# A decoder trunk with expert retrieval: dot products against a PSUM copy of the tokens, and expert values scaled by ScalarE and summed by accumulating transposes

## The reference

```python
q = (xt @ w_q).reshape(t, 8, 2, 128)
s = einsum("thpd,hpnd->thpn", q, sub_keys)          # 128 keys on each of two sides
s1, i1 = top_k(s[:, :, 0], 16); s2, i2 = top_k(s[:, :, 1], 16)
top_s, pos = top_k(all 256 sums s1 + s2, 16)        # idx: 16 of 16384 experts per head
g = softmax(top_s)
a = einsum("cd,chkd->chk", xc, u_tab[idx])          # one dot product per token and expert
out = einsum("chk,chkd->cd", g * gelu(a), v_tab[idx])
```

## Time and profile before

| | |
|---|---|
| median of 3 runs | 1714.5 us (1711.46 to 1718.54) |
| the profiled execution: span from the first to the last instruction | 1705.4 us |
| of the span: TensorE busy | 1427.1 us (84%) |
| GpSimd busy | 1179.6 us (69%) |
| VectorE busy | 1003.6 us (59%) |
| ScalarE busy | 474.8 us (28%) |
| DMA | 619.30 MB, mean 363 GB/s |

### The profile page before, as it was taken

How to read it: one execution, slowest core, us unless ns; L and a number is a source line. 1 busy time by engine, 2 the same in 40 slices (tenths; PEclk the granted TensorE clock), 3 DMA queues, 4 the chain that set the end, 5 groups by cost and what they waited for, 6 DMA issues and landing times.

```text
span 1705.4 us, 18671 instructions
## 1 busy us (share of the span) xinstructions
PE 1427.1 (84%) x5274; PEld 813.2 (48%) x5274; DVE 1003.6 (59%) x2462; ACT 474.8 (28%) x1459; POOL 1179.6 (69%) x1099
## 2 busy tenths in 40 slices
PE   8999887888777899988787799989878877787775
PEld 7887544455442565454344466545444432233332
DVE  3257777767765534537777824654667864444444
ACT  0213233333232222432333321441333231111112
POOL 0027688777777756776777766786777787777774
PEclk9999999999999999999999999989999998999998
DMA  9629999999999999999999999999999999999997
GB/s 336 195 76 355 367 331 334 378 373 354 350 399 403 392 390 393 371 369 390 400 397 384 391 374 389 388 335 370 391 403 333 362 345 370 397 410 410 409 410 301
DMA packets 224237, 619.30 MB, mean 363 GB/s; under 512 B 18913, under 2 KB 90651, under 8 KB 224155
## 3 DMA queue, kind: packets, MB, share of 16 engines
q0 software_dynamic: 147456, 536.94, 82.1%
q1 hardware_dynamic: 76699, 81.36, 14.3%
HBM read 617.17 MB, written 1.05 MB: 363 GB/s over the span
## 4 chain that ended last, share of the span: by engine, by line
PE 35%; POOL 20%; issue 14%; DVE 13%; DMA 11%; ACT 6%; POOLq 1%; SPq 0%; DVEq 0%; ACTq 0%
PE acc L743 17%; PE tile L704 14%; POOL v_ring L483 10%; POOL u_ring L483 10%; DMA u_ring<-in_peer_u_dram,idx_now 9%; DVE u_ring L939 5%; ACT diag L564 3%; DMA v_ring<-in_peer_v_dram,idx_now 2%; ACT gelus L558 2%; PE tile L840 1%; PE tile L726 1%; PE tile L867 1%; DVE cand L1200 0%; DVE cand L1205 0%; DVE picked L1207 0%
## 5 line engine op out<-in xcount | busy, mean ns | idle before, releaser
L743 PE MATMUL acc<-v_ring,diag 128*128 128x512 f32 x2032 | 962.2, 625 | 147.5 <-DMA v_ring<-in_peer_v_dram,idx_now 101.3
L939 DVE CUSTOM_DVE_ANT_0 u_ring<-u_ring,xffn 128x1024 f32<-128x1024 f32 x512 | 605.6, 1222 | 273.1 <-DMA u_ring<-in_peer_u_dram,idx_now 272.3
L483 POOL DMA_INDIRECT v_ring<-in_peer_v_dram,idx_now x512 | 579.8, 1132 | 206.1 <-issue 127.1
L743 PEld LDWEIGHTS acc<-v_ring,diag 128*128 128x128 f32 x2032 | 392.2, 200 | 688.1 <-issue 670.6
L483 POOL DMA_INDIRECT u_ring<-in_peer_u_dram,idx_now x512 | 574.9, 1123 | 192.4 <-issue 131.7
L550 ACT ACTIVATE gelus<-dots 128x8 f32<-128x8 f32 x64 | 13.4, 209 | 783.3 <-DVE dots L939 783.3
L564 ACT ACTIVATE diag<-ident,gelus 128x128 f32<-128x128 f32 x512 | 156.5, 388 | 2.1
L704 PEld LDWEIGHTS tile<-fT,w_ring 128*128 128x128 f32 x960 | 113.8, 195 | 19.8 <-issue 11.0
L704 PE MATMUL tile<-fT,w_ring 128*128 128x128 f32 x960 | 114.7, 279 | 7.9 <-DVE fT L1065 7.9
L1171 DVE MAX8 topv<-tile 128x8 f32<-128x128 f32 x64 | 15.9, 290 | 165.3 <-PE tile L840 165.3
L558 ACT ACTIVATE gelus<-gelus,gates 128x1 f32<-128x1 f32 x512 | 102.0, 281 | 4.8 <-ACT gelus L550 3.1
(11 more groups left out here) (145 smaller groups left out, 953.4 us busy)
## 6 DMA issues: line engine op xcount, KB each, us to landing
w_ring<-in_peer_wq_dram SPq DMA_DIRECT2D x23, 1024.0 KB, 16.6
w_ring<-in_w_out_dram SPq DMA_DIRECT2D x12, 1024.0 KB, 19.3
w_ring<-in_w_kv_dram SPq DMA_DIRECT2D x12, 1024.0 KB, 16.6
u_ring<-in_peer_u_dram,idx_now POOLq DMA_INDIRECT x512, 7.2
v_ring<-in_peer_v_dram,idx_now POOLq DMA_INDIRECT x512, 7.1
w_ring<-in_w_in_b_dram SPq DMA_DIRECT2D x8, 1024.0 KB, 23.5
u_ring<-in_w_in_a_dram SPq DMA_DIRECT2D x4, 1024.0 KB, 12.6
w_ring<-in_w_mem_kv_dram SPq DMA_DIRECT2D x4, 1024.0 KB, 14.3
```

Of the source, the lines that this page charges most:

```text
L483: pool.indirect_dma_start(ring[:, s, :], None, rows_[:, :], bass.IndirectOffsetOnAxis(idx_now[:, column + s:column + s + 1], 0), element_o ...
L743: ins = pe.matmul(acc[:, 512 * n:512 * n + 512], diag[:, par * G + s, :], v_ring[:, s, 512 * n:512 * n + 512], start=False, stop=False, sk ...
L939: dve.tensor_tensor_reduce(u_ring[:, s, :], u_ring[:, s, :], xffn[:, ph % 2, :], 1.0, 0.0, ALU.mult, ALU.add, dots[:, par * G + s:par * G ...
```

## The change

Three things are changed together.

1. **Dot products.** At the start of a phase VectorE copies `xffn` into a PSUM tensor `xf` of two banks (`place_row`), and the 8 x 16 dots of the phase read `xf` instead of `xffn`. To make room, there are 4 `tile` banks instead of 6 from the first `ffn` step on; before that step `xf` serves as banks 4 and 5.
2. **Values.** ScalarE no longer writes `diag`. It waits for `v_landed[s]`, scales the whole v slot in place (128x1024), and TensorE adds it by 8 transposes of 128x128 which accumulate in `acc`. So `acc` holds the sum transposed, block by block. The seed of `acc` (the residual stream) is also written by 8 transposes.
3. **The sum.** Since `acc` is transposed, a new step `sum` copies it to `xn`, transposes it back by 8 transposes into two tile banks, and copies (in the last phase adds) the two halves into `xres`. It stands among the steps of group 0 of phases 1, 2 and 3, and at the end.

```diff
-NT = 6
+NT = 4
+NT_START = 6
...
         @block.scalar
-            def group(q, par, ph, head):
+            def group(q, par, ph, head, slots=G):
...
                 act.wait_ge(gelu_done, q + 1)
-                if not (isinstance(q, int) and q < 2):
-                    act.wait_ge(v_added, G * q - G)
...
                 act.wait_ge(act_done, G * q + G)
-                for s in range(G):
-                    act.activation(diag[:, par * G + s, :], ident[:, :], ACT.Copy,
-                                   scale=gelus[:, par * G + s:par * G + s + 1]).then_inc(diag_made, 1)
+                for s in range(slots):
+                    act.wait_ge(v_landed[s], 16 * q + 16)
+                    act.activation(v_ring[:, s, :], v_ring[:, s, :], ACT.Copy,
+                                   scale=gelus[:, par * G + s:par * G + s + 1]).then_inc(v_scaled, 1)
...
         @block.tensor
-                for n in range(2):
-                    pe.matmul(acc[:, 512 * n:512 * n + 512], ident[:, :], xres[:, ph % 2, 512 * n:512 * n + 512],
-                              start=True, stop=False, skip_group_check=True)
+                for k in range(KD):
+                    pe.matmul(acc[:, P * k:P * k + P], xres[:, ph % 2, P * k:P * k + P], ident[:, :],
+                              start=(k % 4 == 0), stop=False, is_transpose=True, skip_group_check=True)
...
-                    pe.wait_ge(diag_made, G * q + s + 1)
-                    pe.wait_ge(v_landed[s], 16 * q + 16)
-                    for n in range(2):
-                        ins = pe.matmul(acc[:, 512 * n:512 * n + 512], diag[:, par * G + s, :],
-                                        v_ring[:, s, 512 * n:512 * n + 512], start=False, stop=False,
-                                        skip_group_check=True)
+                    pe.wait_ge(v_scaled, G * q + s + 1)
+                    for k in range(KD):
+                        ins = pe.matmul(acc[:, P * k:P * k + P], v_ring[:, s, P * k:P * k + P], ident[:, :],
+                                        start=False, stop=False, is_transpose=True, skip_group_check=True)
                     ins.then_inc(v_added, 1)
...
+                elif kind == "sum":
+                    ph = step[1]
+                    pe.wait_ge(acc_read, ph + 1)
+                    for i in range(2):
+                        transposes(("xs", ph, i), [xn[:, P * k:P * k + P] for k in range(4 * i, 4 * i + 4)])
...
         @block.vector
-                    dve.tensor_tensor_reduce(u_ring[:, s, :], u_ring[:, s, :], xffn[:, ph % 2, :], 1.0, 0.0,
+                    dve.tensor_tensor_reduce(u_ring[:, s, :], u_ring[:, s, :], xf[:, :], 1.0, 0.0,
                                              ALU.mult, ALU.add, dots[:, par * G + s:par * G + s + 1])\
...
+            def place_row(ph):
...
+                dve.tensor_copy(xf[:, :], xffn[:, ph % 2, :]).then_inc(xf_made, 1)
```

More of the change, by code:

```diff
@@ L127, in make_schedule @@
     side[2, 0] += [("route", 2, 7)]
-    side[3, 0] += [("route", 3, 7), ("final", 0)]
+    side[3, 0] += [("route", 3, 7), ("sum", 2), ("final", 0)]
     return pe_start, start, side
@@ L167, in step_tiles, with place_tiles @@
         return [("q", *step[1:]), ("sc", *step[1:])]
+    if kind == "sum":
+        return [("xs", step[1], i) for i in range(2)]
     return []
-STEPS = PE_START + [s for ph in range(PHASES) for g in range(GROUPS) for s in SIDE[ph, g]]
+STEPS = PE_START + [s for ph in range(PHASES) for g in range(GROUPS) for s in SIDE[ph, g]] + [("sum", PHASES - 1)]
 TILES = [t for s in STEPS for t in step_tiles(s)]
 TILE = {t: n for n, t in enumerate(TILES)}
+def place_tiles():
+    bank, turn, last = {}, {}, [-1] * NT_START
+    count = [0] * NT_START
+    for n, t in enumerate(TILES):
+        open_banks = range(NT_START if n < TILE["fT", 0, 0] else NT)
+        b = min(open_banks, key=lambda i: last[i])
+        bank[t], turn[t] = b, count[b]
+        last[b] = n
+        count[b] += 1
+    return bank, turn, count
+BANK, TURN, USES = place_tiles()
 ROUTES = [s[1:] for s in STEPS if s[0] == "route"]
@@ L268, in trunk @@
         probT = sb("probT", [P, 2, 4, P])
-        diag = sb("diag", [P, 2 * G, P])
+        rows = sb("rows", [P, P])
         TAIL = CONV_K - 1
@@ L312, in trunk @@
         acc = ctx.enter_context(nc.psum_tensor("acc", [P, D], F32))
+        xf = ctx.enter_context(nc.psum_tensor("xf", [P, D], F32))
         banks = [ctx.enter_context(nc.psum_tensor(f"tile{i}", [P, 512], F32)) for i in range(NT)]
+        banks += [xf[:, 512 * i:512 * i + 512] for i in range(NT_START - NT)]
         x_landed = [sem(f"x_landed{i}") for i in range(NCH)]
@@ L328, in trunk @@
         tile_filled = sem("tile_filled")
-        tile_emptied = [sem(f"tile_emptied{i}") for i in range(NT)]
+        tile_emptied = [sem(f"tile_emptied{i}") for i in range(NT_START)]
+        xf_made = sem("xf_made")
         head_filled = sem("head_filled")
@@ L356, in bank @@
         def bank(key):
-            return banks[TILE[key] % NT]
+            return banks[BANK[key]]
         def filled(eng, key):
@@ L680, in _ @@
                     side(step)
-            with act.Fori(1, GROUPS // 2) as i:
+            with act.Fori(1, GROUPS // 2 - 1) as i:
                 for par in range(2):
                     group(i * 2 + (base + par), par, PHASES - 1, i)
+            group(base + GROUPS - 2, 0, PHASES - 1, GROUPS // 2 - 1)
+            group(base + GROUPS - 1, 1, PHASES - 1, GROUPS // 2 - 1, PE_LAST)
             root(("final", 1))
@@ L692, in take @@
                 assert next(order) == key, key
[L693 to L696, removed]
+                if TURN[key]:
+                    pe.wait_ge(tile_emptied[BANK[key]], TURN[key])
+                return banks[BANK[key]]
             def done(ins):
@@ L752, in side @@
                     t = take(("gains",))
-                    done(pe.transpose(t[:, 0:NROW], diag[0:NROW, 0, :], ident[0:NROW, 0:NROW]))
+                    done(pe.transpose(t[:, 0:NROW], rows[0:NROW, :], ident[0:NROW, 0:NROW]))
                     for _ in range(WARM_UP):
@@ L915, in _ @@
                     seed(PHASES - 1)
-                group(base + g, g)
+                group(base + g)
             with pe.Fori(1, GROUPS // 2 - 1) as i:
                 for par in range(2):
-                    group(i * 2 + (base + par), par)
-            group(base + GROUPS - 2, 0)
-            group(base + GROUPS - 1, 1, PE_LAST)
+                    group(i * 2 + (base + par))
+            group(base + GROUPS - 2)
+            group(base + GROUPS - 1, PE_LAST)
+            side(("sum", PHASES - 1))
         @block.vector
@@ L1068, in side @@
                     route(*step[1:])
+                elif kind == "sum":
+                    read_sum(step[1])
                 elif kind == "final":
@@ L1234, in _ @@
             for ph in range(PHASES - 1):
+                place_row(ph)
                 for g in range(GROUPS):
                     group(GROUPS * ph + g, g % 2, ph)
-                    if g == 0 and ph:
-                        read_sum(ph - 1)
                     for step in SIDE[ph, g]:
@@ L1242, in _ @@
             base = GROUPS * last
+            place_row(last)
             for g in range(2):
                 group(base + g, g, last)
-                if g == 0:
-                    read_sum(last - 1)
                 for step in SIDE[last, g]:
```

47 lines of the change are left out of this document (31 added, 16 removed).

## The result

The changed kernel takes **2264.73 us** (median of 4 runs, 2262.47 to 2266.29) where the kernel before takes 1712.98 us (4 runs, 1711.35 to 1718.54). The ratio is **1.3208, 95% interval 1.3179 to 1.3237**. The forecast was 2227 us in a range of 2100 to 2350, with 0.96 on slower: sign and range hold, and the time came out 38 us (1.7%) above the forecast. The profiled execution spans 2263.2 us, 557.8 more than the one before.

What follows compares the result with a forecast made beforehand. Bound: a 23.52 us ring of waits through dots, ScalarE and the route step; in phase 3, GpSimd's issue. Terms 380 + 115 + 13 + 15 - 7 - 4 = +512 us on 1705.4, plus 9.1: about 2227 us, range 2100 to 2350.

Steps and rivals of the forecast that it cites:

- the main term: Groups with a route step and no attention: ScalarE's wait for slot 7 adds 13.1 us in each of 29, 380 us.
- Landed at S + 25.8 ... ScalarE is free at S + 26.8: Route group, S its first dot: slot 7's V row lands, its scaling ends, ScalarE free at S + 26.8 instead of S + 13.66.
- the clock rival: TensorE's clock stays low after idling, so score matmuls and transposes slow; up to 2362 us, put at 2310; chance 0.12.
- 13.1 - 6.7 = 6.4, 18 x 6.4 = 115: Attention groups of phases 1 and 2: the wait less the relief from shorter adding, 6.4 us each, 115 us over 18.
- In the 18 attention groups (9 each in phases 1 and 2) TensorE is on the path: Attention groups: TensorE's adding is on the path, so shortening it takes 6.7 us per group off the wait.
- I take 8.1: Groups with steps: a fetch takes 8.1 us from issue to landing, the median beside weight loads.
- The bound is GpSimd's issue: Phase 3, which has no steps: GpSimd's issuing of fetches bounds a group, at 8 x 2.56 us.
- The -7 us: Phase 3, 14 groups: u issues fall from 1.01 to 0.94 us, saving 7 us if the DMA engines can take it.
- the end (-4): End of the kernel: shorter transposes remove the last fetches' waits for slots to be added, 8 x 0.48, saving 4 us.
- The operand doesn't free GpSimd: Rival: with dots reading PSUM, GpSimd's issues stay stretched and slot 7 comes later; 139 us more, 2366 us; chance 0.06.
- ScalarE's own work: Rival: landings don't matter, only ScalarE's scalings count, +5.6 us per route group; 156 us more, 1870 us; chance 0.04.
- Faster: Rival: ScalarE keeps up with its steps and TensorE's relief remains; 1598 us; chance 0.03.

Runs made afterwards that it cites:

- kernel 1: The changed kernel with ScalarE's 8 scalings, and their waits, moved behind its steps; 1653.66 us, ratio 0.9617 to the kernel before.
- kernel 2: The kernel before with one line added: ScalarE waits for v_landed[s] ahead of each diagonal; 2393.09 us.
- kernel 7: The changed kernel with four scalings ahead of ScalarE's steps and four behind, so pq waits for slot 3 instead of slot 7; 1797.11 us.
- kernel 3: The changed kernel with ScalarE scaling only the first 128 of the 1024 columns of each V slot; 2233.28 us.
- kernel 5: The kernel before with only the dots reading xf in PSUM, place_row and four tile banks, diagonals kept; 1683.4 us, ratio 0.9819.
- kernel 4: The changed kernel with dots reading xffn in SBUF again instead of xf in PSUM; 2387.53 us.

## Why the prediction was right

**The mechanism and the main term.** The step "Landed at S + 25.8 ... ScalarE is free at S + 26.8" reads S + 27.16 in the group shown, and "issued at S + 17.7" reads S + 17.67. Over the 29 route groups without attention ScalarE is free at S + 27.8 in the mean (25.3 to 32.5), against S + 14.1 before. Kernels 1, 2 and 7 show by subtraction, addition and dose that this wait is the loss. From first dot to first dot the 29 route groups without attention took 392 us more, 13.5 each, against 380 and 13.1.

**The scaling** took 1.145 us, not 1.0. With a scale, 128 columns take 0.400 us (kernel 3) and 1024 take 1.145: 0.83 ns a column and 0.29 us besides, where the plain copies that I drew my line through leave 0.17 us. What I left out is probably the scale that is read from SBUF; the copies also read PSUM, and no run separates the two. The Trainium skill, ScalarE: Activation LUTs, section What ACT_TABLE_LOAD costs, has a fixed part, 0.833 ns per column and some 93 ns for each per-partition operand, 1.13 us here; the trace agrees, at 1.145.

**The score matmul** took 1.19 us instead of 0.68. This was in the clock rival and not in the forecast. In all 32 steps the score matmuls' busy time went from 25.3 to 37.7 us, 12 us more.

**The attention groups are the term that was mis-sized.** "13.1 - 6.7 = 6.4, 18 x 6.4 = 115" came out at 159 us, 44 too many: 74.4 in phase 1, 85.0 in phase 2. From first dot to first dot (groups of a phase counted from 0):

- Groups 1 and 3 shrank, by 0 to 6.1 us, and groups 2 and 4 behind them grew, by 11 to 19. Taken in pairs they grew by 5.6, 13.1, 11.0 and 14.5 us, 44 together, where the forecast had 51.
- The two groups 0 grew by 12.2 and 15.1 us, 14.5 together above the forecast; `sum` and `place_row`, which the forecast counts apart, are in them.
- Groups 5 to 8 grew by 87.9 us in all, 11.0 each, where the forecast had 6.4. That is 37 of the 44 us.

Here is group 5 of phase 1, before and after:

```profile
671.68 1.22 DVE L939 CUSTOM_DVE_ANT_0 u_ring<-u_ring,xffn 128x1024 f32<-128x1024 f32 x1
...
684.25 2.45 ACT L564 ACTIVATE diag<-ident,gelus 128x128 f32<-128x128 f32 x8
...
690.50 14.00 PE L743 MATMUL acc<-v_ring,diag 128*128 128x512 f32 x32
...
692.62 1.22 DVE L939 CUSTOM_DVE_ANT_0 u_ring<-u_ring,xffn 128x1024 f32<-128x1024 f32 x1
```

```profile
894.83 1.22 DVE L965 CUSTOM_DVE_ANT_0 u_ring<-u_ring,xf 128x1024 f32<-128x1024 f32 x1
...
920.00 1.15 ACT L585 ACTIVATE v_ring<-v_ring,gelus 128x1024 f32<-128x1024 f32 x1 [1.41 <-DMA v_ring<-in_peer_v_dram,idx_now]
...
925.30 9.09 PE L764 MATMUL acc<-ident,v_ring 128*128 128x128 f32 x64
...
926.92 1.22 DVE L965 CUSTOM_DVE_ANT_0 u_ring<-u_ring,xf 128x1024 f32<-128x1024 f32 x1
```

ScalarE is done with its part of the group at S + 15.0 before and at S + 26.3 after, and the next dot comes 5.9 and 5.8 us behind that. The adding begins 2 us before that dot and runs on beside the next group's dots, in both kernels. The whole 11.3 us of the wait arrive, and the shorter adding (9.1 us instead of 14.0) gives nothing back. Over the eight groups ScalarE is done 10.7 us later in the mean, and the groups are 11.0 us longer. So the step that failed is "In the 18 attention groups (9 each in phases 1 and 2) TensorE is on the path": it took 6.7 us of relief off groups in which the adding holds nothing up. The wait there was 2.4 us smaller than the 13.1 put, which hid part of it.

Landings varied too. In group 4 of phase 1 the last scalings begin at 849.94, 853.35 and 856.71, 3.4 us apart instead of 2.6, while the DMA engines move 395 GB/s (842 to 857) with weights among it; so "I take 8.1" is one median for landings that differ with what else is on its way. But this group and the short one before it grew by 13.1 us together, against 12.8 forecast, so the missing time isn't there.

**Phase 3's reason was wrong, its time right.** "The bound is GpSimd's issue" doesn't hold after the change. The issues are free now, 0.94 us every 1.24, and a group still takes 20.5 us. The timeline in phase 3, and the fetches into `v_ring` there (to be laid beside the earlier trace rows):

```profile
2060.02 0.94 POOL L505 DMA_INDIRECT u_ring<-in_peer_u_dram,idx_now  x1 [0.30 <-issue]
...
2061.26 0.94 POOL L505 DMA_INDIRECT v_ring<-in_peer_v_dram,idx_now  x1 [0.30 <-issue]
...
2061.78 1.22 DVE L965 CUSTOM_DVE_ANT_0 u_ring<-u_ring,xf 128x1024 f32<-128x1024 f32 x1 [1.34 <-DMA u_ring<-in_peer_u_dram,idx_now]
...
2064.33 1.22 DVE L965 CUSTOM_DVE_ANT_0 u_ring<-u_ring,xf 128x1024 f32<-128x1024 f32 x1 [1.32 <-DMA u_ring<-in_peer_u_dram,idx_now]
```

```profile
DMA to landing us min/median/max: 5.6/9.5/12.2
```

GpSimd issues a pair every 2.48 us, the dots come every 2.55, and the median landing grew from 6.6 to 9.5 us: the fetches queue in the DMA engines. A pair is 1.05 MB, which in 2.56 us is 410 GB/s, the figure of the page's slices there. At 2.56 us a pair the kernel before moved 410 GB/s too, so that the time came out unchanged is luck: I named a limit of the same size. The -7 us that I made conditional ("if the DMA engines can take it") wasn't there in the steady groups, and the end (-4) took 0.8 us more. The phase without its first group still shrank by 8.6 us, against 11 forecast, but the gain came in its groups 2 to 4, 9.6 us for which no term stands: luck again, and its cause is open.

**The small terms.** `place_row` took 1.22 us four times, as put. The extra for banks wasn't looked at by itself; kernel 5 contains it and is faster. `sum` has no measurement of its own either.

**The rivals.** *Clock:* its mechanism is real, its price was too high. The granted clock is 0.70 to 0.71 in the phases with steps and 0.66 in the last, where it was 0.96 and 0.91; but in the route group shown the 64 transposes took 8.16 us, not 13. Kernel 2, which idles likewise but adds by matmuls, has 0.76 to 0.78 in its phases with steps, so most of the fall there comes without transposes. In the last phase both have the same fetches, and kernel 2 is granted 0.91 with TensorE busy 79% of the time, the changed kernel 0.67 with 63%: the steady stretch of that phase, of kernel 2 and then of the changed kernel, columns as above.

```profile
2080.00:2330.00 250.00, 196.56 (x384) 76.22 (x384) 117.89 (x192) 60.12 (x207) 192.68 (x206) 0.91 1.02 402
```

```profile
1950.00:2180.00 230.00, 144.41 (x729) 124.80 (x728) 114.37 (x189) 119.55 (x187) 175.52 (x195) 0.67 1.02 406
```

The Trainium skill, TensorE: Matmul & The Clock Gate, section PE-mode transpose, says that the fast clock doesn't engage for transposes. The low clock of this phase fits that, but 64 transposes in a row at 784.70, behind matmuls, were granted 1.00 and took 7.15 us, so it doesn't hold as a rule here. In phase 3 fewer busy microseconds and transposes come together, and no run separates them. The low clock cost nothing in the last phase of kernel 1, which is granted 0.66 too and moves 410 GB/s. *The operand doesn't free GpSimd:* fell. Of the 1024 issues 231 took over 1.1 us before, 8 do after (the longest 1.84), and 211 in kernel 4. The Trainium skill, GPSIMD Engine Reference, section Key points (contention with two SBUF inputs), is borne out: 0.94 against up to 1.99 us. *ScalarE's own work:* fell with kernels 1 and 3 (its terms add up to 154 us, not 156). *Faster:* it needed ScalarE free before S + 13.7. I had looked for that in the fetches alone, but the order of ScalarE's program gives it too, and kernel 1 is that case.

## What to carry to other kernels

Before a wait for a transfer goes into an engine that works in order, list what is queued behind it and who waits for that: the step behind this wait needed nothing of the transfer, and it held up four engines for some 13 us a group with a route step. Put short work that others wait for ahead of work that waits for landings, and try that order before a change is judged by its time, since the same parts gave 1.32 times and 0.96 times the time before. And an order is good only with its parts: the same one cost the kernel with the 14 us adding 7%.

## What the runs showed of the hardware

- The fetches of 4 KB rows settle at 410 GB/s in the phase without steps, before and after the change and in eight of the nine experiments (kernel 4 stays at 368 to 389). With issues every 1.24 us instead of 1.28 the pairs still come every 2.55 us, and the median landing grows from 6.6 to 9.5 us. The Trainium skill, DMA: Bandwidth & Descriptors, section Specifications, gives 435 GB/s as the fabric's ceiling; no slice of a page here came above 410.
- A dot with both inputs in SBUF holds a GpSimd issue to as much as 1.99 us, one with an input in PSUM leaves it at 0.94, and the dot takes 1.22 us either way.
- 64 accumulating fp32 transposes took 8.16 us where TensorE had idled before (granted clock 0.88 over them) and 7.15 us in an attention group where it had been busy (1.00); eight took 1.09 us at 2.4 GHz and 1.97 us at 1.2.

What stays open is whether the transposes or the lower busy share hold the clock low in phase 3, what made its groups 2 to 4 shorter, and what bounds kernel 1.
